# Where the side projection's matmul steps are dealt inside a DeltaNet head

## The chip, the cores and the metric

The kernel runs on one core of a Trainium2 chip. The metric is the device time of one execution in microseconds; the kernel before takes 2391.67 us, the median of three runs (2391.39 to 2391.86).

## The reference, cut to what matters

One layer of a hybrid trunk over 128 context tokens and 1024 latent tokens, D_MODEL = 1024, all in float32. One input projection feeds a pooling mixer, merge gates and a bidirectional chunked gated DeltaNet with 8 heads of width 128; an expert mixture with 16 experts follows. The change lies in the DeltaNet heads:

```python
decay = jnp.exp(jnp.where(incl, g[..., :, None] - g[..., None, :], -jnp.inf))
k_beta = k * beta[..., None]
lmat = jnp.where(strict, jnp.einsum('bhnck,bhnsk->bhncs', k_beta, k) * decay, 0.0)
a = lmat + jnp.eye(CHUNK, dtype=jnp.float32)
rhs = jnp.concatenate([v * beta[..., None], k_beta * jnp.exp(g)[..., None]], axis=-1)
sol = lax.linalg.triangular_solve(a, rhs, left_side=True, lower=True, unit_diagonal=True)
...
def step(S, inp):
    u_c, w_c, q_c, k_c, attn_c, d_c = inp
    v_new = u_c - jnp.einsum('bhck,bhkv->bhcv', w_c, S)
    o_c = (jnp.einsum('bhck,bhkv->bhcv', q_c, S) + jnp.einsum('bhcs,bhsv->bhcv', attn_c, v_new))
    S = S * d_c[..., None, None] + jnp.einsum('bhck,bhcv->bhkv', k_c, v_new)
    return S, o_c
```

The triangular solve is done in the kernel by inverting a unit triangular 128x128 matrix of each of 9 token tiles, in each direction, by block doubling.

## The kernel before, in words

The program is written by hand for each engine and synchronised by semaphores. After a prologue (adaLN, norms, the first head's projections) there are eight DeltaNet heads, seven in a hardware loop and a last one with its own table, then output projections, merge and the experts.

A head has two kinds of TensorE (PE) work. The first is its own chain: L2 norms and transposes of q, k, v, the products k k and k q (L1016), the inversion, its correction ("res" and "fix"), and a scan of nine token tiles (L1080 to L1105). The second is side work that nothing of this head waits for until late: the projections of the next head's q, k, v and this head's gate (pairs "qv" and "kg"), and two tiles of the merge and pooling columns (pair "AB"). `project` is a generator that yields after each matmul of it. Such a yield is a step; a step over 512 columns is L823 and shows in the trace as two matmul records, a step over 128 columns is L809. A pair is cut into jobs: two of 128 columns and eight steps each (c0, c1), and seven of 512 columns and four steps each, run in the order 1, 2, 6, 7, 5, 4, 3. Of these 1, 6, 7, 3 are copied out of PSUM by ScalarE (ACT, L863) and 2, 5, 4 are added by VectorE (DVE, L871), at the places where `evac` and `add` stand in those engines' programs. A job may begin only when the job before the last has left its bank.

`fill(place)` in `body_pe` runs as many steps as belong to a place. `FILL` gives each place a budget in units of 512 columns, and `steps_until` turns the running sum into step counts. The order of the places is the order of the program; the number of steps in all, 132 in a loop head and 156 in the last, is fixed, and what the budgets leave is run at the last place, "end2".

The inversion goes through six levels, b = 2, 4, 8, 16, 32, 64. The nine tiles stand in three groups g = 0, 1, 2, each with a PSUM bank of its own for either direction. On PE a level is, in float16:

- for each g a product Z (L1031, three matmuls) and, above the first level, a transpose X (L1023, three); then `fill("Z{b}_{g}")`;
- for each g a product P (L1031, three); then `fill("P{b}_{g}")`.

Z of group g waits for `low_changed` of the level below (L1043), X waits for `up_changed`, and P waits for ACT's copies of Z and X (L1209). DVE closes the level with nine operations in a fixed order: join 0 (L1402, reads P of group 0 from PSUM), to_low 0 (L1409), join 1, to_up 0 (L1414), to_low 1, join 2, to_up 1, to_low 2, to_up 2. Ahead of join 0 stands `add("Z{b}_2")`, which adds every sum job that is complete by that place. to_low g releases Z of the next level, to_up g releases X.

At a head's end the last scan tile is followed by `fill("end1")`, `fill("end2")`, and then nine transposes (L1124) of the normed output, which wait for DVE's L1497. The chain to it is: ACT drains the outputs, GpSimd (POOL) adds and squares them (L1598, L1600), DVE adds the jobs of "end1" and reduces (L1495), ACT takes a logarithm and an exponential, DVE multiplies (L1497). ACT then applies Silu to the gate (L1271) and copies job AB3. The first step of the next head waits until AB3 is copied (L787), and ACT goes on to the next head's Silu (L1145), from which the next head's chain runs through DVE's L1387 to the transposes L1023 that open the inversion ("Y2").

Of the kernel before, what the change touches and what calls it, by code (L numbers as in the profile page):

```python
# [19 lines left out]
P = 128  # L20
# [28 lines left out]
LEVELS = (2, 4, 8, 16, 32, 64)  # L49
# [29 lines left out]
def build(nc, a, out_p, out_s, out_sf, out_sb, dbg=None, stop=99):  # L79
    ctx = ExitStack()  # L80
    with ctx:
# [75 lines left out]
        qT, kT, vT, gateT = qkvg  # L157
# [516 lines left out]
            return [job_cols(job) for job in order for _ in range(job_steps(job))]  # L674

        UNIT = 512
        FILL = {"start": 4, "nk": 2.75, "qT": 4, "kk": 4, "Y20": 1, "Y21": 0.5, "Y22": 0.5, "X0": 1, "X1": 1, "X2": 1, "res": 2, "fix": 4, "end1": 5.5}
        FILL |= {f"{x}{b}_{g}": 0 if b in LEVELS[:3] and (x, g) == ("P", 2) else 1 for b in LEVELS for x in "ZP" for g in range(3)}
        FILL |= {f"scan{t}{x}": 1 for t in range(1, NT) for x in "abc"}
        FILL_LAST = FILL | {"start": 5, "Y20": 3, "Y21": 3, "Y22": 2, "fix": 4, "end1": 8}  # L680
        FILL_LAST |= {f"scan{t}{x}": 2 if x == "b" else 1 for t in range(1, NT) for x in "abc"}
# [3 lines left out]
        def steps_until(order):  # L685

            cols, budget, n, at = step_cols(order), 0.0, 0, {}
            for place in PLACES:
                budget += UNIT * (FILL if order is ORDER else FILL_LAST).get(place, 0)
                while n < len(cols) and sum(cols[:n + 1]) <= budget:  # L690
# [2190 lines left out]
```

## Time and profile before

| | |
|---|---|
| median of 3 runs | 2391.67 us (2391.39 to 2391.86) |
| the profiled execution | 2394.42 us, its span 2392.7 us |
| PE busy | 2302.0 us, 96% |
| DVE, ACT, POOL busy | 1101.9, 932.4, 380.4 us |
| a loop head (seven of them) | 132.7 us |
| the last head | 149.6 us |
| granted clock of PE, mean | 0.989 |

The profiled execution is 2.75 us above the median of the runs. A busy share of 96% for PE says little by itself: the ends of matmuls are modelled, so that a short wait between two groups may not show as idle time. The starts of the rows are the surer reading. All times below are from the start of the span.

### The profile page before, as it was taken

What the parts mean: (1) busy time and instruction counts of PE and PEld (TensorE: products, weight loads), DVE (VectorE), ACT (ScalarE), POOL (GpSimd) and SP (SyncE); (2) the same over time, 40 slices, a digit from 0 to 9 for tenths busy, and PEclk for the clock granted to TensorE, in tenths of its full rate; (3) what the DMA queues carried; (4) which work ended last, traced back from release to release, by engine and by line L of the source; (5) the groups of instructions that cost most, each with busy time, mean ns of one, the idle gap of its engine ahead of it and who ended that gap; (6) DMA issues with size and microseconds to landing.
All of it is one profiled execution on the core that took longest, in us unless ns stands there. A gap on an engine that the chain in (4) does not pass through costs nothing.

```text
span 2392.7 us, 39733 instructions
## 1 busy us (share of the span) xinstructions
PE 2302.0 (96%) x14208; PEld 1684.7 (70%) x14208; DVE 1101.9 (46%) x2161; ACT 932.4 (39%) x2437; POOL 380.4 (16%) x270
## 2 busy tenths in 40 slices
PE   6999999999999999999999999779999999999997
PEld 3456566665756666665644444569999999999997
DVE  3587776868686776866235316720010000100003
ACT  4173746555473747455311123213222232222323
POOL 1040413122230404132100000001001010010101
PEclk9999999999999999999999999979999999999999
DMA  9610212120201202121342422368877888778885
GB/s 346 253 47 22 68 38 69 35 72 18 86 21 42 61 24 69 29 70 40 143 161 99 159 79 106 121 219 294 295 250 261 281 293 296 250 260 282 293 291 213
DMA packets 198882, 362.31 MB, mean 151 GB/s; under 512 B 9082, under 2 KB 72519, under 8 KB 195723
## 3 DMA queue, kind: packets, MB, share of 16 engines
q1 hardware_dynamic: 191994, 341.73, 41.0%
q0 software_dynamic: 6528, 19.47, 3.1%
q8 instruction: 36, 0.59, 0.1%
q14 instruction: 51, 0.42, 0.1%
q10 hardware_dynamic: 273, 0.11, 0.0%
HBM read 320.63 MB, written 40.65 MB: 151 GB/s over the span
## 4 chain that ended last, share of the span: by engine, by line
PE 87%; DVE 5%; issue 3%; ACT 3%; DMA 1%; DVEq 0%; SPq 0%; ACTq 0%; POOLq 0%; POOL 0%
PE bank L823 22%; PE bank L2537 21%; PE bank L2551 11%; PE bank L2150 5%; PE bank L1887 5%; PE bank L1031 3%; PE bank L801 3%; PE bank L1905 2%; PE bank L1023 2%; PE bank L1089 2%; PE bank L809 1%; PE bank L1100 1%; PE bank L1105 1%; PE bank L1104 1%; PE bank L1080 1%
## 5 line engine op out<-in xcount | busy, mean ns | idle before, releaser
L823 PE MATMUL bank<-arena 128*128 128x512 f32 x1344 | 675.4, 606 | 0.0
L2537 PE MATMUL bank<-arena 128*128 128x144 f32 x4096 | 514.2, 286 | 3.1 <-ACT arena L2571 3.1
L2537 PEld LDWEIGHTS bank<-arena 128*128 128x128 f32 x4096 | 510.9, 190 | 3.2 <-ACT arena L2571 3.2
L2644 DVE TENSOR_TENSOR arena<-arena,bank 128x144 f32<-128x144 f32 x128 | 39.2, 306 | 698.9 <-ACT arena L2585 698.9
L823 PEld LDWEIGHTS bank<-arena 128*128 128x128 f32 x1344 | 217.0, 191 | 88.8 <-issue 87.5
L2551 PE MATMUL bank<-arena 128*128 128x144 f32 x2048 | 257.3, 286 | 0.7 <-DVE arena L2644 0.7
L2551 PEld LDWEIGHTS bank<-arena 128*128 128x128 f32 x2048 | 253.8, 189 | 1.9 <-DVE arena L2644 0.9
L2585 ACT ACTIVATE arena<-bank 128x144 f32<-128x144 f32 x128 | 37.5, 293 | 461.7 <-PE bank L2537 461.7
L1031 PEld LDWEIGHTS bank<-arena 128*128 128x128 f16 x1296 | 96.4, 98 | 156.4 <-issue 137.7
L1209 ACT ACTIVATE arena<-bank 128x384 f16<-128x384 f16 (+1 forms) x360 | 159.8, 491 | 90.0 <-PE bank L1031 67.9
L863 ACT ACTIVATE arena<-bank 128x128 f32<-128x128 f32 (+1 forms) x156 | 75.9, 491 | 169.5 <-PE bank L823 107.7
L1294 DVE SCALAR_TENSOR_TENSOR arena<-arena 128x1156 f32<-128x1156 f32 x96 | 136.1, 1417 | 1.3
L2150 PE MATMUL bank<-arena 128*128 128x512 f32 x288 | 128.7, 601 | 4.1 <-DVE arena L2044 2.1
L1303 POOL TENSOR_TENSOR arena<-arena 128x512 f32<-128x512 f32 x68 | 94.7, 1401 | 188.8 <-DVE arena L1512 60.4
L1031 PE MATMUL bank<-arena 128*128 128x128 f16 x1296 | 120.8, 219 | 1.9 <-DVE arena L1409 1.9
L1242 ACT ACTIVATE arena<-bank,arena 128x128 f32<-128x128 f32 x144 | 53.5, 371 | 151.4 <-PE bank L1089 151.4
L1887 PE MATMUL bank<-arena 128*128 128x512 f32 x256 | 110.6, 592 | 1.3 <-DVE arena L1510 1.3
L1402 DVE CAST_PREDICATED arena<-arena,bank 128x384 f16<-128x384 uint32 x144 | 79.7, 553 | 64.1 <-PE bank L1031 64.1
L2150 PEld LDWEIGHTS bank<-arena 128*128 128x128 f32 x288 | 53.8, 192 | 68.5 <-issue 66.4
L809 PEld LDWEIGHTS bank<-arena 128*128 128x128 f32 x768 | 92.4, 191 | 8.9 <-issue 6.2
L1409 DVE COPY_PREDICATED arena<-arena 128x384 f16<-128x384 uint32 x144 | 94.7, 657 | 6.9 <-DVE arena L1402 0.9
L809 PE MATMUL bank<-arena 128*128 128x128 f32 x768 | 97.7, 276 | 0.0
(327 smaller groups left out, 3038.3 us busy)
## 6 DMA issues: line engine op xcount, KB each, us to landing
arena<-in_exp_w_gate SPq DMA_DIRECT2D x32, 2048.0 KB, 10.6
arena<-in_exp_w_up SPq DMA_DIRECT2D x32, 2048.0 KB, 15.5
arena<-in_exp_w_down SPq DMA_DIRECT2D x32, 2048.0 KB, 10.8
arena<-in_w_in SPq DMA_DIRECT2D x52, 512.0 KB, 5.3
arena<-in_ada_w SPq DMA_DIRECT2D x24, 1024.0 KB, 8.1
side_dram<-arena SPq DMA_DIRECT2D x20, 576.0 KB, 4.2
arena<-g_dram SPq DMA_DIRECT2D x16, 576.0 KB, 4.2
arena<-in_x_sample SPq DMA_DIRECT2D x16, 512.0 KB, 6.0
```

The source lines that it names most:

```text
L809: ins = nc.tensor.matmul(bank[:, 0:CTX], weights_of(name)[:, k, :], hT3[:, k, 0:CTX], start=(k == 0), stop=(k == KD - 1))
L823: ins = nc.tensor.matmul(bank[:, 0:LH], w[:, k, :], x[:, k, :], start=(k == 0 and job[2] in "127"), stop=(k == KH - 1), skip_group_check=( ...
L1031: last = nc.tensor.matmul(TRI[d][g][:, i * P:(i + 1) * P], lhs[:, 3 * g + i, :], rhs[:, 3 * g + i, :], start=(n == 0), stop=(n == len(term ...
L1209: nc.scalar.activation(flat(dst, g), src[:, 0:384], ACT.Copy).then_inc(sem(f"drained{d}_act"), 1)
L1294: ins = nc.vector.scalar_tensor_tensor(conv_to[j][:, 0:CW], raw[j][:, tap:tap + CW], w, conv_to[j][:, 0:CW], ALU.mult, ALU.add)
L1303: unit.tensor_tensor(out, x, y, op).then_inc(sem("sums_ready"), 1)
L1402: nc.vector.copy_predicated(up[:, 3 * g:3 * g + 3, :], masks[:, 0, lv + 1, :].unsqueeze(1).to_broadcast([P, 3, P]), TRI[1][g][:, 0:384].re ...
L1409: nc.vector.copy_predicated(low[:, 3 * g:3 * g + 3, :], rows, up[:, 3 * g:3 * g + 3, :]).then_inc(sem("low_changed"), 1)
L1887: last = nc.tensor.matmul(banks[n % RING][:, 0:CH], w_dn[half][:, k, col:col + P], bT3[:, k, CTX + c * CH:CTX + (c + 1) * CH], start=(k == ...
L2150: last = nc.tensor.matmul(banks[2 * (i % 2) + half][:, 0:512], mixT3[:, k, t * P:(t + 1) * P], w_outs[:, k, half * 512:(half + 1) * 512], ...
L2537: last = nc.tensor.matmul(banks[3 + f % 2][:, m * CAP:(m + 1) * CAP], w_unit[2 * half + m][:, k, col:col + P], xsT[:, k, :], start=(k == 0 ...
L2551: last = nc.tensor.matmul(banks[5 + dt % 2][:, 0:CAP], w_unit[4 + half][:, k, col:col + P], hid[:, k, :], start=(k == 0), stop=(k == KD - 1))
```

## The change

Only the table `FILL` changes, and with it `FILL_LAST`, which is built from it. At the six levels the budgets per group go from 1, 1, 1 at Z to 0, 1, 2 (1, 0, 2 at b = 16), and at P from 1, 1, 1 (1, 1, 0 at b = 2, 4, 8) to 0, 2, 1 (0, 2, 0 at b = 8 and 0, 2, 2 at b = 64). "kk" goes from 4 to 5. A loop head then has run 86 steps instead of 82 when its scan begins, and "end2" holds 4 steps instead of 8; in the last head 5 instead of 9.

```diff
-        FILL = {"start": 4, "nk": 2.75, "qT": 4, "kk": 4, "Y20": 1, "Y21": 0.5, "Y22": 0.5, "X0": 1, "X1": 1, "X2": 1, "res": 2, "fix": 4, "end1": 5.5}
-        FILL |= {f"{x}{b}_{g}": 0 if b in LEVELS[:3] and (x, g) == ("P", 2) else 1 for b in LEVELS for x in "ZP" for g in range(3)}
+        FILL = {"start": 4, "nk": 2.75, "qT": 4, "kk": 5, "Y20": 1, "Y21": 0.5, "Y22": 0.5, "X0": 1, "X1": 1, "X2": 1, "res": 2, "fix": 4, "end1": 5.5}
+        FILL |= {f"Z{b}_{g}": n for b in LEVELS for g, n in enumerate((1, 0, 2) if b == 16 else (0, 1, 2))}
+        FILL |= {f"P{b}_{g}": n for b in LEVELS for g, n in enumerate((0, 2, 0) if b == 8 else (0, 2, 2) if b == 64 else (0, 2, 1))}
```

The new table is one line longer, so every line number behind it is higher by one in the changed kernel.

PE, loop head, from P of group 1 at b = 4 to X of group 1 at b = 8, in the kernel before (bank4 and bank5 hold P of groups 1 and 2, bank0 and bank1 hold Z, bank3 and bank4 hold X, bank7 the side steps):

```order
L1031 MATMUL bank4<-arena 128x128 x3
L823 MATMUL bank7<-arena 128x512
L1050 REGISTER_ALU
L631 REGISTER_ALU
L1031 MATMUL bank5<-arena 128x128 x3
L1043 ISA
L1031 MATMUL bank0<-arena 128x128 x3
L1023 MATMUL bank3<-arena 128x128 x3
L823 MATMUL bank7<-arena 128x512
L1043 REGISTER_ALU
L1031 MATMUL bank1<-arena 128x128 x3
L1023 MATMUL bank4<-arena 128x128 x3
```

The same stretch in the changed kernel:

```order
L1032 MATMUL bank4<-arena 128x128 x3
L824 MATMUL bank7<-arena 128x512 x2
L1051 REGISTER_ALU
L631 REGISTER_ALU
L1032 MATMUL bank5<-arena 128x128 x3
L750 REGISTER_ALU
L824 MATMUL bank6<-arena 128x512
L1044 ISA
L1032 MATMUL bank0<-arena 128x128 x3
L1024 MATMUL bank3<-arena 128x128 x3
L1044 REGISTER_ALU
L1032 MATMUL bank1<-arena 128x128 x3
```

Two steps now stand between P of groups 1 and 2 and one before Z of group 0, and none is left between X of group 0 and Z of group 1.

DVE, loop head, the end of level b = 4 and the begin of b = 8, before (L871 adds a sum job, here qv5, L1402 with bank3 is join 0 of b = 8):

```order
L1409 COPY_PREDICATED arena<-arena 128x384
L1414 COPY_PREDICATED arena<-arena 128x384
L868 REGISTER_ALU
L869 REGISTER_ALU
L871 TENSOR_TENSOR arena<-arena,bank7 128x512
L619 REGISTER_ALU
L1402 COPY_PREDICATED arena<-arena,bank3 128x384
```

and in the changed kernel:

```order
L1410 COPY_PREDICATED arena<-arena 128x384
L1415 COPY_PREDICATED arena<-arena 128x384
L869 REGISTER_ALU
L870 REGISTER_ALU
L872 TENSOR_TENSOR arena<-arena,bank7 128x512
L869 REGISTER_ALU
L870 REGISTER_ALU
L872 TENSOR_TENSOR arena<-arena,bank6 128x512
L1403 COPY_PREDICATED arena<-arena,bank3 128x384
```

Two sum jobs stand there now, qv5 (bank7) and qv4 (bank6); qv4 used to be added one level later. Its last step is now the last of `fill("Z8_2")`, the one directly ahead of P of group 0.

PE, end of a loop head, the changed kernel, from the last scan product to the transposes L1125:

```order
L1106 MATMUL bank5<-arena 128x128
L824 MATMUL bank7<-arena 128x512 x3
L750 REGISTER_ALU
L824 MATMUL bank6<-arena 128x512 x4
L822 REGISTER_ALU
L824 MATMUL bank7<-arena 128x512 x4
L1125 MATMUL bank0<-arena 128x128 x3
```

These are 11 steps (the ends of AB5, AB4 and AB3), where the kernel before has 15 at this place.

## Rows read from the trace of the kernel before

**Rows 1.** Page part 4 and stretches: us, then busy us (instructions) of each engine

```profile
PE 87%; DVE 5%; issue 3%; ACT 3%; DMA 1%; DVEq 0%; SPq 0%; ACTq 0%; POOLq 0%; POOL 0%
...
382.58:515.26 132.68, 130.81 (x759) 82.94 (x758) 98.93 (x180) 75.11 (x190) 34.64 (x22) 1.00 0.16 48
```

**Rows 2.** Stretches of that head, between starts of Y2, the levels' P, X, res

```profile
406.10:412.20 6.10, 6.07 (x37) 3.25 (x38) 5.03 (x9) 5.69 (x15) 4.11 (x4) 1.00 0.00 0
412.20:419.66 7.46, 6.61 (x38) 3.25 (x37) 5.45 (x9) 4.89 (x13) 2.33 (x4) 1.00 0.00 0
419.66:426.16 6.50, 6.44 (x38) 3.25 (x37) 5.18 (x10) 4.97 (x13) 1.05 (x1) 1.00 0.00 0
426.16:432.71 6.55, 6.47 (x38) 3.29 (x37) 5.08 (x10) 4.19 (x11) 2.27 (x2) 1.00 0.00 0
...
439.73:446.75 7.02, 7.02 (x40) 3.59 (x39) 6.23 (x11) 4.28 (x12) 2.91 (x2) 1.00 0.10 24
446.75:450.00 3.25, 3.25 (x16) 1.54 (x15) 2.81 (x5) 1.02 (x3) 2.09 (x1) 1.00 0.00 0
```

**Rows 3.** Timeline of PE: start us, us, engine, line, operation [idle before]

```profile
419.68 0.33 PE L1031 MATMUL bank<-arena 128*128 128x128 f16 x3
419.86 1.07 PE L823 MATMUL bank<-arena 128*128 128x512 f32 x2
420.77 0.33 PE L1031 MATMUL bank<-arena 128*128 128x128 f16 x3
...
423.82 0.34 PE L1023 MATMUL bank<-arena 128*128 128x128 f16 x3
...
456.03 1.94 PE L823 MATMUL bank<-arena 128*128 128x512 f32 x4
457.80 1.21 PE L1031 MATMUL bank<-arena 128*128 128x128 f16 x18
```

**Rows 4.** Timeline of DVE, levels 2 to 8 of that head

```profile
413.42 1.52 DVE L1409 COPY_PREDICATED arena<-arena 128x384 f16<-128x384 uint32 x1
...
420.17 0.56 DVE L1402 CAST_PREDICATED arena<-arena,bank 128x384 f16<-128x384 uint32 x1 [1.71 <-PE bank L1031]
...
421.81 0.56 DVE L1414 COPY_PREDICATED arena<-arena 128x384 f16<-128x384 uint32 x1
...
423.21 0.55 DVE L1414 COPY_PREDICATED arena<-arena 128x384 f16<-128x384 uint32 x1
...
424.38 0.56 DVE L1414 COPY_PREDICATED arena<-arena 128x384 f16<-128x384 uint32 x1
425.12 0.69 DVE L871 TENSOR_TENSOR arena<-arena,bank 128x512 f32<-128x512 f32 x1 [0.17 <-PE bank L823]
```

**Rows 5.** Timeline of POOL at the same place

```profile
413.26 1.27 POOL L1303 TENSOR_TENSOR arena<-arena 128x512 f32<-128x512 f32 x1
```

**Rows 6.** Timeline of PE, end of that head and begin of the next

```profile
502.19 13.05 PE L823 MATMUL bank<-arena 128*128 128x512 f32 x30
515.09 1.15 PE L1124 MATMUL bank<-arena 128*128 128x128 f32 x9
516.11 3.83 PE L809 MATMUL bank<-arena 128*128 128x128 f32 x32
...
538.80 0.51 PE L1023 MATMUL bank<-arena 128*128 128x128 f16 x6 [0.77 <-DVE arena L1387]
```

**Rows 7.** Timeline of DVE, the same

```profile
510.97 1.36 DVE L1497 TENSOR_TENSOR arena<-arena 128x1152 f32<-128x1152 f32 x1 [0.61 <-ACT arena L1264]
```

**Rows 8.** Timeline of ACT, the same

```profile
512.25 1.26 ACT L1271 ACTIVATE arena<-arena 128x128 f32<-128x128 f32 x2
515.29 0.60 ACT L863 ACTIVATE arena<-bank 128x512 f32<-128x512 f32 x1 [1.77 <-PE bank L823]
515.91 1.28 ACT L1145 ACT_TABLE_LOAD   x1
```

**Rows 9.** Waits of PE over six loop heads: us in all, times, longest

```profile
PE bank L1023 <- DVE arena L1387: 4.6, 6, 0.8
```

## The prediction

> **What bounds the kernel now.** I read the chain that ended last first: 87% of the span is PE [rows 1]. The number of matmuls doesn't change, so the time can only move through what lies between them. Then one loop head, cut into stretches: it lasts 132.68 us at a granted clock of 1.00 throughout [rows 1], and five of the six others last as long within 0.05 us; the first has the prologue ahead of it. Within it I cut at the start of each level's first P [rows 2]. A level with five steps takes 6.50 or 6.55 us, one with six takes 7.02 (two stretches alike, one shown), and the first boundary takes 7.46. Last I read PE and DVE row by row at those cuts, since the waits sit in the gaps between starts.
>
> **The units.** Fifteen steps in a row take 515.09 - 502.19 = 12.90 us, 0.86 each [rows 6]. A group of three float16 matmuls takes 419.86 - 419.68 = 0.18, and 0.17 where starts are compared over more groups; I use 0.17. A lone step between float16 groups takes 420.77 - 419.86 = 0.91, and two together 457.80 - 456.03 = 1.77 [rows 3]. So each interruption by steps costs about 0.05 us beside the steps, which is the one thing that dealing them in twos saves. A loop head's levels have 33 interruptions before and 23 after, a gain of 10 x 0.05 = 0.5 us, contained in the walks below.
>
> [...]
>
> **What the levels wait for.** DVE's nine operations start 0.49 us after P of group 0 starts (420.17 against 419.68) and run at a fixed pace. Counted from that start of P, to_up 0 ends at 421.81 + 0.56 - 419.68 = 2.69, to_up 1 at 4.08, to_up 2 at 5.26 [rows 3, 4]. X of group 1 starts at 423.82 - 419.68 = 4.14, 0.06 behind its release [rows 3]; by the same 0.06 X of group 0 can start at 2.75. Before, a five-step level already touches this chain, and a six-step level doesn't. X of group 2 can't start before 5.32.
>
> Now the walk of a changed level with six steps (0, 2, 1 at P and then 0, 1, 2 at Z). P0, P1, two steps, P2, one step, Z0, X0: X0 starts at 0.17 + 0.17 + 1.77 + 0.17 + 0.91 + 0.17 = 3.36, no wait. Z1 at 3.53, X1 would come at 3.70 and must wait until 4.14: 0.44 us, since the step that stood between X0 and Z1 is gone. Then 4.14 + 0.17 + 0.91 + 0.17 = 5.39 for X2, no wait, 5.56 its end, and two steps more before the next P0: 7.33 us. The two steps behind X2 are the point: P0 opens the next DVE chain, and they now stand in series with the old one.
>
> **Part by part, a loop head, net of steps at 0.86.** (A step run here isn't run at the end.)
> - Y2 to P of b = 2, five steps either way: walk 6.03 against 6.10, -0.07.
> - b = 2 to 4. POOL's L1303 stretches to_low 0 to 1.52 us, 0.96 more than its 0.56 [rows 4, 5]; both start as before, so X1 comes at 4.14 + 0.96 = 5.10. After: 5.10 + 0.17 + 0.91 + 0.34 + 1.77 = 8.29 with six steps, 3.13 net; before 7.46 - 4.30 = 3.16. -0.03.
> - b = 4 to 8: 7.33 - 5.16 = 2.17 against 6.50 - 4.30 = 2.20. -0.03.
> - b = 8 to 16, five steps. The add of qv4 now stands before join 0 and its last step ends only as P0 starts. An add starts about 0.20 behind its step (425.12, where the step behind X of 423.82 ends at 423.82 + 0.17 + 0.91 = 424.90) and DVE is free again some 0.60 later [rows 3, 4], so join 0 starts at 0.80 instead of 0.49 and X2 at 5.63. With 0, 2, 0 at P and 1, 0, 2 at Z, PE waits for DVE at X0, X1, Z2 and X2. 5.63 + 0.17 + 1.77 = 7.57, 3.27 net, against 6.55 - 4.30 = 2.25. +1.02. If the add hides wholly this is +0.7.
> - b = 16 to 32 and 32 to 64: 7.33 against 7.02, six steps both: +0.31 each.
> - P of 64 to X: three groups and four steps in two pairs, 4.05 - 3.44 = 0.61, against 3.25 - 2.58 = 0.67. -0.06.
>
> Sum +1.45 us a loop head, 10.2 for seven. Bounds: 0 each if every new wait is hidden (then -0.5 by the interruptions), 2.2 if each level still loses another 0.15. In the last head the walk is much the same, with more adds and longer POOL operations among the joins: 1.45, bounds -0.5 and +3.
>
> **The head's end.** L1497 ends at 510.97 + 1.36 = 512.33 [rows 7]; the steps end at 515.09, so the transposes wait for nothing [rows 6]. With 11 steps these end at 502.19 + 9.46 = 511.65. The add of AB4 joins that of AB5 before the reduction, but its last step is the seventh as AB5's was, so the reduction stays where it is. The transposes start at 512.38, a wait of 0.73, and end at 513.40. ACT's Silu of the gate ends at 513.51 [rows 8], the AB3 copy at about 514.05, and the next head's first step, which needs it, starts at 514.1 instead of 516.11: a second wait of 0.7. What is late next: ACT starts the next head at 514.07 instead of 515.91, 1.84 earlier, and before, the inversion opened on ACT's and DVE's chain with a 0.77 us wait [rows 6], six times 4.6 us together [rows 9]. So it opens at 538.80 - 1.84 = 536.96. PE, with one step more at "kk", gets there at 514.1 + (538.03 - 516.11) + 0.86 = 536.9: the old wait is used up. Net: 1.8 us earlier for three steps (2.58 us) fewer, +0.78, in six of the seven transitions. Into the last head, where PE had no such wait, the loss is whole: 3.44 saved at the end, 2.0 kept, +1.4. The first head loses a 0.28 wait: -0.3. At the last head's own end 14 steps stay before the transposes and cover the chain. Together 6 x 0.78 + 1.4 - 0.3 = +5.8 us. Bounds: -0.3 if the tail's chain moves forward with the steps, +9 if none of the old 0.77 is recovered.
>
> The scan keeps one budget unit per place; which places have the short steps moves by three, at equal columns. DVE's add of kg5 goes between "res" and "fix", where DVE idled 0.8 us; AB2's goes two tiles earlier, beside idle time. I cost both at nothing; uncovered, each is 0.6 us a head. Loads on SP's queue that follow a job are issued earlier or, at the end, up to 2 us earlier; nobody waits for them.
>
> **Sum.** 10.2 + 1.45 + 5.8 = +17.4 us on the profiled execution of 2394.42, 2411.8. The median is 2.75 below that execution, so 2409.1 for the median.
>
> **Rivals.**
> - *Only the levels.* The head's end is covered because the reduction moves forward. For it: POOL was done before the add. Against: the add waits for the same seventh step. 2391.7 + 11.4 = 2403.
> - *Only the head's end.* The levels' steps cover DVE wherever they stand, as the 7.02 us levels suggest with no wait at all. Against: X of group 1 starting 0.06 behind its release in level 4. 2391.7 + 5.8 - 8 x 0.5 = 2393.5, no change that can be measured.
> - *Faster.* Pairs run without gaps and DVE's chain isn't tied to P of group 0: with P0 and P1 back to back, join 0 and join 1 are ready together, and the chain is ahead by the time Z0 comes; all waits behind L1387, 4.6 us, go too. Place: the six levels; price: -0.5 a head and up to -1.0 of the gaps at the five-step levels; it decides if X of group 2 is released by 4.5 us instead of 5.26 after P0. 2391.7 - 8 x 0.5 - 4.6 = 2383. For it: X0 no longer waits at b = 4 and 8. Against: the nine operations already run without a gap once join 0 has started.
>
> **How the numbers follow.** Both parts as walked: 0.63, 2409, own range 2403 to 2415. Only the levels 0.12; only the end 0.08; faster 0.12; anything else 0.05. The range 2396 to 2415 holds the first two and part of the rest. A difference under 0.2%, 4.8 us, can't be told from none. Slower by more: 0.63 + 0.12 + some of the rest, 0.80; faster by more 0.13; within 0.07.
>
> **What would show it.** In the profile after: six-step levels of 7.33 us between starts of P0, with X of group 1 waiting 0.4 for L1415; 7.6 for b = 8 to 16, with an L872 between P0 and join 0; 0.7 us idle ahead of L1125 and again ahead of the next head's first step; no wait for L1388 ahead of the inversion; a loop head of about 134.9 us. Levels of 6.9 would refute the first part, a head's end with no idle PE the second.

## The result and the profile after

The changed kernel takes 2410.57 us (median of 4 runs, 2409.27 to 2412.11), the kernel before 2391.77 beside it (2391.39 to 2392.04). The ratio is 1.0078, interval 1.0064 to 1.0092: slower by 0.8%. The profiled execution of after is the run of 2409.27, its span 2407.5.

The chain of waits of this profile breaks off half way (PE has 50% of the span in it, against the 87% of [rows 1]), so I compare stretches. First the whole loop head and its levels, cut where [rows 1] and [rows 2] cut it: us, then busy us of PE, PEld, DVE, ACT and POOL (instructions), granted clock, DMA.

```profile
385.25:520.08 134.83, 130.86 (x758) 83.08 (x758) 100.49 (x180) 74.21 (x191) 33.53 (x22) 1.00 0.16 47
409.73:415.78 6.05, 6.05 (x38) 3.29 (x38) 5.04 (x9) 5.64 (x14) 4.06 (x4) 1.00 0.00 0
415.78:424.14 8.36, 7.43 (x40) 3.67 (x39) 5.50 (x9) 5.68 (x15) 2.37 (x4) 1.00 0.00 0
424.14:431.49 7.35, 7.09 (x40) 3.66 (x39) 5.08 (x10) 4.10 (x11) 1.90 (x1) 1.00 0.00 0
431.49:439.09 7.60, 6.67 (x38) 3.33 (x37) 5.09 (x10) 5.11 (x12) 2.15 (x2) 1.00 0.00 0
446.44:453.79 7.35, 7.08 (x40) 3.66 (x39) 6.54 (x11) 3.94 (x11) 2.73 (x2) 1.00 0.00 0
453.79:457.85 4.06, 4.06 (x18) 1.96 (x17) 3.93 (x6) 0.97 (x2) 0.66 (x1) 1.00 0.00 0
457.85:461.60 3.75, 3.75 (x25) 2.04 (x24) 3.60 (x6) 2.60 (x6) 0.00 (x0) 1.00 0.00 0
```

PE's busy time is the same as before (130.86 against 130.81), and 2.15 us were added to the head: all of it is waiting. A six-step level takes 7.35 where it took 7.02, and the one from b = 8 to 16 takes 7.60 with five steps where it took 6.55. The last row is X to "res": 3.75, where before it was 3.97 (450.00 to 453.97).

PE's timeline in levels 8 and 16, the rows that answer to [rows 3]; a wait stands in brackets:

```profile
428.31 0.34 PE L1024 MATMUL bank<-arena 128*128 128x128 f16 x3 [0.26 <-DVE arena L1415]
...
431.87 1.93 PE L824 MATMUL bank<-arena 128*128 128x512 f32 x4
433.64 0.51 PE L1032 MATMUL bank<-arena 128*128 128x128 f16 x6
434.59 0.34 PE L1024 MATMUL bank<-arena 128*128 128x128 f16 x3 [0.44 <-DVE arena L1415]
...
437.17 0.34 PE L1024 MATMUL bank<-arena 128*128 128x128 f16 x3 [0.36 <-DVE arena L1415]
```

The reader is to see that PE stands at X each time (L1024, released by to_up, L1415), that the wait printed at b = 8 comes right behind a Z with no step between, and that P of groups 0 and 1 is followed by two steps in one piece. The printed waits are short by the modelled ends: that Z started at 427.71, so X of group 1 stood for 428.31 - 427.71 - 0.17 = 0.43 us, the 0.44 of the walk. DVE at the same place ([rows 4] before; the first row is to_up 2, the end of the chain that began with P of b = 4 at 424.14):

```profile
428.87 0.56 DVE L1415 COPY_PREDICATED arena<-arena 128x384 f16<-128x384 uint32 x1
...
431.72 0.69 DVE L872 TENSOR_TENSOR arena<-arena,bank 128x512 f32<-128x512 f32 x1 [1.70 <-PE bank L824]
432.33 0.55 DVE L1403 CAST_PREDICATED arena<-arena,bank 128x384 f16<-128x384 uint32 x1
```

The add stands between P of group 0 (431.49) and join 0, which starts 0.84 behind P and not 0.49.

The head's end: PE, then DVE, then ACT ([rows 6 to 8] before).

```profile
520.08 1.20 PE L1125 MATMUL bank<-arena 128*128 128x128 f32 x9 [0.58 <-DVE arena L1498]
521.91 3.83 PE L810 MATMUL bank<-arena 128*128 128x128 f32 x32 [0.63 <-ACT arena L864]
...
544.60 0.51 PE L1024 MATMUL bank<-arena 128*128 128x128 f16 x6
```

```profile
518.66 1.36 DVE L1498 TENSOR_TENSOR arena<-arena 128x1152 f32<-128x1152 f32 x1 [0.61 <-ACT arena L1265]
```

```profile
519.94 1.26 ACT L1272 ACTIVATE arena<-arena 128x128 f32<-128x128 f32 x2
521.11 0.58 ACT L864 ACTIVATE arena<-bank 128x512 f32<-128x512 f32 x1
```

The transposes wait for DVE's multiply, the next head's first step waits for ACT's copy, and the inversion (544.60) opens without the wait that it had in [rows 6]. By starts the first of these waits is 0.74 us: the eleven steps start at 509.88 and need 9.46. PE's waits over six loop heads, in answer to [rows 9] (us in all, times, longest):

```profile
PE bank L1024 <- DVE arena L1415: 14.4, 42, 0.6
PE bank L1125 <- DVE arena L1498: 4.1, 7, 0.6
PE bank L810 <- ACT arena L864: 3.8, 6, 0.6
```

### The profile page after: what moved, and what is told of

Same layout as the page of the kernel before. It is cut to its first block, busy times and chain, and to the rows that moved or that the text cites. A ratio compares the mean times of both kernels' runs of the same rounds, so it can differ in the third digit from the quotient of the medians.

```text
span 2407.5 us, 39734 instructions
## 1 busy us (share of the span) xinstructions
PE 2300.5 (96%) x14208; PEld 1685.0 (70%) x14208; DVE 1113.8 (46%) x2161; ACT 925.8 (38%) x2437; POOL 373.4 (16%) x270
## 4 chain that ended last, share of the span: by engine, by line
PE 50%; DVE 1%; ACT 1%; issue 0%; DMA 0%; POOLq 0%; POOL 0%; DVEq 0%; ACTq 0%
PE bank L2538 21%; PE bank L2552 11%; PE bank L2151 5%; PE bank L1888 5%; PE bank L1906 2%; PE bank L824 2%; PE bank L2160 1%; PE bank L2508 1%; PE bank L2520 1%; DMA arena<-xn_dram,arena 0%; PE bank L1896 0%; PE bank L2178 0%; PE bank L2169 0%; DVE arena L2321 0%; PE bank L2512 0%
## 5 line engine op out<-in xcount | busy, mean ns | idle before, releaser
L824 PE MATMUL bank<-arena 128*128 128x512 f32 x1344 | 658.0, 602 | 0.0
L1032 PEld LDWEIGHTS bank<-arena 128*128 128x128 f16 x1296 | 91.0, 98 | 112.6 <-issue 95.2
L1295 DVE SCALAR_TENSOR_TENSOR arena<-arena 128x1156 f32<-128x1156 f32 x96 | 150.1, 1563 | 1.3
L2151 PE MATMUL bank<-arena 128*128 128x512 f32 x288 | 127.0, 595 | 4.1 <-DVE arena L2045 2.1
L1032 PE MATMUL bank<-arena 128*128 128x128 f16 x1296 | 113.5, 219 | 1.8
L1888 PE MATMUL bank<-arena 128*128 128x512 f32 x256 | 110.6, 592 | 1.3 <-DVE arena L1511 1.3
L1243 ACT ACTIVATE arena<-bank,arena 128x128 f32<-128x128 f32 x144 | 53.5, 371 | 128.7 <-PE bank L1090 128.7
L2151 PEld LDWEIGHTS bank<-arena 128*128 128x128 f32 x288 | 53.2, 189 | 67.5 <-issue 65.3
L2598 ACT ACTIVATE arena<-bank,arena 128x128 f32<-128x128 f32 x128 | 47.2, 369 | 128.5 <-PE bank L2552 128.5
```

Source lines behind the costliest of these rows:

```text
L824: ins = nc.tensor.matmul(bank[:, 0:LH], w[:, k, :], x[:, k, :], start=(k == 0 and job[2] in "127"), stop=(k == KH - 1), skip_group_check=( ...
L1032: last = nc.tensor.matmul(TRI[d][g][:, i * P:(i + 1) * P], lhs[:, 3 * g + i, :], rhs[:, 3 * g + i, :], start=(n == 0), stop=(n == len(term ...
L1295: ins = nc.vector.scalar_tensor_tensor(conv_to[j][:, 0:CW], raw[j][:, tap:tap + CW], w, conv_to[j][:, 0:CW], ALU.mult, ALU.add)
L1888: last = nc.tensor.matmul(banks[n % RING][:, 0:CH], w_dn[half][:, k, col:col + P], bT3[:, k, CTX + c * CH:CTX + (c + 1) * CH], start=(k == ...
L2151: last = nc.tensor.matmul(banks[2 * (i % 2) + half][:, 0:512], mixT3[:, k, t * P:(t + 1) * P], w_outs[:, k, half * 512:(half + 1) * 512], ...
```

## The experiments

Every kernel below differs from the kernel before by the lines shown, unless it says from the changed one. "A head" is the stretch between two starts of the transposes of the tail, the third and fourth heads' ends: 132.68 us before, 134.83 in the changed kernel.

**The deal alone.** The levels dealt in pairs, with the totals of before.

```diff
+        FILL |= {f"Z{b}_{g}": n for b in LEVELS for g, n in enumerate((0, 1, 2))}
+        FILL |= {f"P{b}_{g}": n for b in LEVELS for g, n in enumerate((0, 2, 0) if b <= 8 else (0, 2, 1))}
```

> Only the dealing is changed: Z 0, 1, 2 at every level, P 0, 2, 0 at b = 2, 4, 8 and 0, 2, 1 above, so every level has as many steps as before, and the head's end keeps its 8. Theory (P0 opens the next DVE chain, and the two steps behind X of group 2 stand in series with the old chain): the three five-step boundaries take as long as the six-step ones, about 7.3 us instead of 6.5 (b = 2 to 4: 8.3 instead of 7.5), +0.85 each, the two six-step ones 7.35 instead of 7.02, less about 0.1 elsewhere: +3.0 us a head, +24 for eight, about 2416. Rival (only the head's end costs): 2391.8 or, by the interruptions saved, 2388.

Measured: 2421.44 us, ratio 1.0126 (1.0110 to 1.0141). A head takes 135.59, 2.91 more, and the head's end is as before (its old 0.8 wait for L1388 is there six times). PE at b = 2 to 4 and on:

```profile
419.90 0.35 PE L1032 MATMUL bank<-arena 128*128 128x128 f16 x3 [0.37 <-DVE arena L1410]
420.83 0.34 PE L1024 MATMUL bank<-arena 128*128 128x128 f16 x3 [0.59 <-DVE arena L1415]
421.30 0.34 PE L1032 MATMUL bank<-arena 128*128 128x128 f16 x3
422.23 0.34 PE L1024 MATMUL bank<-arena 128*128 128x128 f16 x3 [0.59 <-DVE arena L1415]
```

So the deal by itself makes the levels slower, with no step added or taken. In three of the seven loop heads something came on top that the theory didn't have: another 1.65 us. PE's granted clock is the last figure but two of each row. The first row is from a head without the loss, the others from one with it:

```profile
419.41:422.41 3.00, 1.33 (x15) 0.70 (x13) 3.00 (x7) 1.69 (x4) 0.01 (x1) 1.00 0.00 0
...
555.00:558.00 3.00, 1.33 (x15) 0.70 (x13) 3.00 (x7) 1.70 (x4) 0.00 (x1) 1.00 0.00 0
...
560.00:561.00 1.00, 1.00 (x4) 0.48 (x3) 0.00 (x0) 1.00 (x3) 0.00 (x0) 0.50 0.00 0
...
562.00:565.00 3.00, 3.00 (x16) 1.38 (x16) 1.67 (x4) 0.60 (x1) 0.00 (x0) 1.00 0.00 0
```

PE was busy for 1.33 of 3.00 us while it waited for L1415, and then its clock was at 0.50 (the 1.2 GHz level) for some 3 us: two steps in a row took 2.88 us (559.98) against 1.94 at the full clock (563.04). Three times 1.65 us is about what this kernel is slower than the theory's figure. In the other four heads PE went through the same waits, to 0.01 us, and the clock stayed at 1.00 (the same two steps took 1.94 us at 423.67). So the waits alone don't decide it, and what does isn't shown.

**The totals alone.** One step per place throughout, 86 steps when the scan begins as in the changed kernel.

```diff
-        FILL |= {f"{x}{b}_{g}": 0 if b in LEVELS[:3] and (x, g) == ("P", 2) else 1 for b in LEVELS for x in "ZP" for g in range(3)}
+        FILL |= {f"{x}{b}_{g}": 1 for b in LEVELS for x in "ZP" for g in range(3)}
```

"kk" is 5 instead of 4 here too.

> The changed kernel's totals per head (36 steps in the levels, kk 5, four taken from the head's end), but dealt one at each of the 36 places. Theory: no level waits for DVE except the first (b = 2 to 4, stretched by POOL); boundaries of 7.0 us with six steps each, net of steps -1.5 us a head against before, -12 for eight, and the head's end +5.8 as in the changed kernel: about 2385.5, faster than before. Rival (the moved steps themselves cost, wherever they are dealt): like the changed kernel, 2410.

Measured: 2389.36 us, 0.9986 (0.9977 to 0.9995). A head takes 132.14: with the same 36 steps in the levels (one more between P of 8 and P of 16, one fewer behind P of 64), the even deal is 2.69 us a head and 21 us in all faster than the changed kernel. It missed its own figure by some 4 us. One cause is seen, and the rest stays open: POOL's attention multiply stretches to_low of group 0 at b = 64 to 1.61 us, where it took 1.31.

**The head's end alone.** Four steps from the end to "fix", the levels untouched.

```diff
-... "fix": 4, "end1": 5.5}
+... "fix": 8, "end1": 5.5}
```

> The levels as before; four steps of a loop head's end go to the place fix (4 to 8), kk stays 4. Theory of the head's end: the transposes wait about 0.6 and the next head's first step about 0.6, the next inversion opens 1.84 us earlier against 3.44 us of steps taken away, and nothing uses up the wait ahead of it: +1.6 us in six transitions and +1.4 into the last head, +11, 2403. Rival (the end is covered): 2391.8.

Measured: 2403.69 us, 1.0049 (1.0035 to 1.0062). A head takes 134.23, 1.55 more: 0.78 at the transposes, 0.78 at the next head's first step. The old wait at the inversion stays:

```profile
542.87 0.51 PE L1023 MATMUL bank<-arena 128*128 128x128 f16 x6 [0.76 <-DVE arena L1387]
```

**The same with one of the four at "kk".**

```diff
-"kk": 4, ... "fix": 4,
+"kk": 5, ... "fix": 7,
```

> As the run before, but one of the four steps goes to kk (5) and three to fix (7), as in the changed kernel. Theory: the step at kk uses the wait ahead of the inversion (0.77 us in six heads, 0.28 in the first): +0.78 x 6 + 1.4 - 0.3 = +5.8, 2397.6. Rival one: the end is covered, 2391.8. Rival two: the wait at the inversion isn't recovered, 2403 as the run before.

Measured: 2403.86 us, 1.0053 (1.0039 to 1.0067), a miss by 6 us, and the theory of the rival isn't right either. The wait at the inversion is gone as expected (24.51 us from the transposes to the inversion, 384.28 to 408.79, with a step more). The 0.8 us come back behind P of b = 64. The sum job kg2 is complete one place earlier, so DVE adds it at the end of b = 32, ahead of its convolution tap (L1294, a product and sum over 1156 columns for the next head's convolution). DVE and then POOL:

```profile
447.55 0.68 DVE L871 TENSOR_TENSOR arena<-arena,bank 128x512 f32<-128x512 f32 x1
448.14 3.42 DVE L1294 SCALAR_TENSOR_TENSOR arena<-arena 128x1156 f32<-128x1156 f32 x1
```

```profile
447.71 2.63 POOL L1581 TENSOR_TENSOR arena<-arena 128x1152 f32<-128x1152 f32 x1 [4.07 <-DVE arena L1414]
```

The tap starts 0.43 behind POOL's L1581, stands until about that one's end (450.34) and then takes its own 1.42 (the sum would be 3.62, 0.20 more than measured): join 0 of b = 64 is 1.6 late, 2.10 behind its P instead of 0.49. The next kernel tests this.

**Tap first.** The kernel just told, with DVE's two lines exchanged:

```diff
-                add(f"P{b}_2")
                 if lv >= 3:
                     tap()
+                add(f"P{b}_2")
```

> As the kernel with kk 5 and fix 7, but DVE does its convolution tap ahead of the add at the ends of levels 16, 32 and 64. There the add came first in level 32, the tap started 0.43 us behind POOL's L1581 and took 3.42 instead of 1.42 us. Theory (whoever of DVE and POOL starts first keeps the memory port, and the other stands still until it has finished): the tap starts 0.16 ahead of POOL and takes 1.42, join 0 of b = 64 is on time, 0.83 us a head come back in seven heads: 2403.9 - 5.5 = 2398.4. Rival: the 0.77 us at the inversion's start was never to be won, something else in the chain takes it: 2403.9.

Measured: 2398.06 us, 1.0025 (1.0016 to 1.0034). Forecast 2398.4. A head takes 133.38. The tap and POOL's L1581:

```profile
445.82 1.42 DVE L1294 SCALAR_TENSOR_TENSOR arena<-arena 128x1156 f32<-128x1156 f32 x1
```

```profile
445.99 3.74 POOL L1581 TENSOR_TENSOR arena<-arena 128x1152 f32<-128x1152 f32 x1 [4.05 <-DVE arena L1414]
```

Now DVE starts 0.17 ahead, and POOL is the one that is stretched, from 2.63 to 3.74. The order of two operations on one engine, 0.4 us apart, is worth 5.8 us. The Trainium skill ("SBUF — State Buffer", "🔬 SBUF: two separate sides") says that the pair of ports shared by DVE and GpSimd is an exclusive lock: a DVE operation with two SBUF inputs, as this tap is, and a GpSimd operation that reads SBUF exclude each other, whichever starts first has the pair for the whole instruction, and the other fully blocks. The rows of the two kernels agree, from both sides, within 0.2 us.

**Changed kernel, levels made even.** Same totals; P of 8 to 0, 2, 1, Z of 16 to 0, 1, 2, P of 64 to 0, 2, 1. From the changed kernel:

```diff
-enumerate((1, 0, 2) if b == 16 else (0, 1, 2))
+enumerate((0, 1, 2))
-enumerate((0, 2, 0) if b == 8 else (0, 2, 2) if b == 64 else (0, 2, 1))
+enumerate((0, 2, 1))
```

> The changed kernel with the same totals (41 steps in the levels), but P of b = 8 at 0, 2, 1, Z of b = 16 at 0, 1, 2 and P of b = 64 at 0, 2, 1: every level from b = 8 on has six steps in the same order. Theory (a level lasts as long as X of group 1 or 2 is held by DVE, plus what stands behind it): the b = 8 to 16 level loses its wait at X2 because a step now covers it, X of group 1 waits 0.7 instead; walked, 0.4 us a head less, 2407 in all. If it is only the count of steps that matters: 2410.6, unchanged. If the pairs themselves are the cost: 2410.6 or above, since there is one more pair followed by a lone step.

The levels hold 36 steps in both kernels; the 41 of the expectation count the five of "kk" with them. Measured: 2408.74 us, 1.0068 (1.0054 to 1.0082). A head takes 134.38, 0.45 less than in the changed kernel (forecast 0.4); over the whole kernel the difference, 1.8 us, is within the intervals of the two. In the 8 to 16 level PE has one printed wait:

```profile
435.03 0.34 PE L1024 MATMUL bank<-arena 128*128 128x128 f16 x3 [0.59 <-DVE arena L1415]
```

**Changed kernel, qv4's add behind the joins.**

```diff
-                add(f"Z{b}_2")
+                if last_h or b != 8:
+                    add(f"Z{b}_2")
                 join(0)
```

> The changed kernel, with the add of qv4 at b = 8 to 16 moved behind the joins of b = 16 (loop heads only). Theory: the add ahead of join 0 costs 0.31 us a head, so 2410.6 - 7 x 0.31 = 2408.4, and the idle time ahead of X in that level falls to the 0.44 of the other levels. Rival one: the add hides wholly in DVE's gaps, unchanged at 2410.6. Rival two: the bank that qv4 holds comes free some 5 us later and a side step waits for it, 2412 or more.

The expectation says "behind the joins of b = 16", but the edit is at b = 8: the add leaves its place between P of 8 and join 0 and comes behind the nine operations of the same level, at 436.41. Measured: 2406.91 us, 1.0061 (1.0047 to 1.0075). A head takes 134.55, and the 8 to 16 level 7.29 where it took 7.60: the 0.31 us of the walk. Over the whole kernel it is 3.7 us, forecast 2.2, and the intervals of the two kernels overlap. No side step waited for the bank.

```profile
431.22:438.51 7.29, 6.67 (x39) 3.33 (x37) 5.08 (x10) 5.06 (x12) 2.14 (x2) 1.00 0.00 0
```

**A better table, first attempt.** Six steps at b = 2 and 8 too, and the tap first as in "Tap first": 84 steps when the scan begins.

```diff
-"kk": 4, ... "fix": 4,
+"kk": 5, ... "fix": 3,
-0 if b in LEVELS[:3] and (x, g) == ("P", 2) else 1
+0 if b == 4 and (x, g) == ("P", 2) else 1
```

> The kernel before with kk 5 and fix 3, the missing step put in at P of group 2 of b = 2 and b = 8 (only b = 4 stays at five steps), one step per place everywhere else, and DVE's tap ahead of its add. 84 steps when the scan begins, 6 in end2. Theory: six-step levels with ones need 7.02 us and no wait, so the two filled levels win their waits, 1.17 us a head by the walk, and the step at kk wins the 0.77 at the inversion's start in six heads; 13 steps at the head's end still cover the chain there. 2392.2 - 8 x 1.17 - 6 x 0.77 = 2378, say 2375 to 2384. Rival one: the head's end has no room for two steps fewer, 0.8 a head are lost there, 2384 or more. Rival two: to_low of group 0 at b = 64 is stretched by POOL more than before (as with ones everywhere, 1.61 instead of 1.31 us), 0.25 a head lost, 2380.

Measured: 2391.22 us, 0.9996 (0.9987 to 1.0005), a miss by 13 us. PE's waits over six loop heads:

```profile
PE bank L823 <- DVE arena L871: 6.3, 6, 1.1
PE bank L1100 <- DVE arena L1455: 3.8, 6, 0.6
PE bank L1100 <- ACT arena L1243: 1.7, 6, 0.3
```

All waits at X and at the inversion are gone, as walked, and three new ones stand elsewhere, 2 us a head. A side step waits for kg2's bank, since the add now stands behind the tap; two adds stand between "fix" and the scan, ahead of L1455; and a place in the scan whose single step is a short one (0.22 us) doesn't cover ACT. None is a matter of how many steps a level has. All three come from which job ends at which place.

**Second attempt.** Six steps at b = 2 only, so 83 when the scan begins; otherwise as the first.

```diff
-"kk": 4, ... "fix": 4,
+"kk": 5, ... "fix": 3,
-0 if b in LEVELS[:3] and (x, g) == ("P", 2) else 1
+0 if b in LEVELS[1:3] and (x, g) == ("P", 2) else 1
```

> The kernel before with kk 5, fix 3, the missing step put in at P of group 2 of b = 2 alone, and DVE's tap ahead of its add: 83 steps when the scan begins, 7 in end2. In v1 (84 steps) two waits came in that the walk didn't have: a side step waited 1.05 us for the add of kg2 behind the tap, and the scan lost 0.9 us because two adds stand between fix and the remainder of tile 1 and a single short step stands ahead of L1100. With 83 steps kg4's add falls in the scan again, the short step stands elsewhere, and kg2's bank is wanted 1.25 us later. Theory: none of the three losses is there; per loop head 0.92 is won at b = 2 to 4 and 0.77 at the inversion's start, a loop head lasts 131.0 instead of 132.68; 2391.9 - 7 x 0.92 - 6 x 0.77 = 2380.8. Rival (such gains are always taken back by the next thing on the chain): 2388 or more.

Measured: 2382.24 us, 0.9957 (0.9943 to 0.9971): faster than both kernels, 9.7 us less than before and 28 less than the changed one. The profile lists no wait of PE over the six loop heads, and a head takes 131.11, forecast 131.0:

```profile
379.14:510.25 131.11, 130.86 (x758) 82.99 (x757) 99.17 (x180) 74.56 (x190) 34.64 (x22) 1.00 0.16 49
```

**Pairs at P, ones at Z.** As the second attempt, but P 0, 2, 1 (0, 2, 0 at b = 4 and 8).

```diff
+        FILL |= {f"Z{b}_{g}": 1 for b in LEVELS for g in range(3)}
+        FILL |= {f"P{b}_{g}": n for b in LEVELS for g, n in enumerate((0, 2, 0) if b in LEVELS[1:3] else (0, 2, 1))}
```

> As v2_step_at_2_kk5_fix3, but the two steps of P of groups 0 and 1 stand together behind group 1 (0, 2, 1 at P; 0, 2, 0 at b = 4 and 8) and Z keeps 1, 1, 1. Theory (what costs in the changed kernel is that two steps stand behind X of group 2 and none between X of 0 and X of 1, not that steps stand in pairs): no wait is added, and one interruption of 0.05 us a level is saved, 0.25 to 0.3 us a head, 2 us in all less than v2: 2379. Rival (the pairs at P delay or disturb DVE's chain as much as those at Z): the six-step levels of 7.3 us come back, 2385 or more.

Measured: 2381.42 us, 0.9960 (0.9947 to 0.9974), a head 131.07. Pairs at P cost nothing that can be measured. A six-step level takes 6.96 (429.06 to 436.02) where it takes 7.02 in the second attempt (430.53 to 437.55), which is the interruption saved; most of it is lost again at X, 0.16 at b = 4 and about 0.2 behind b = 64, and the whole is no measurable gain.

**Taps at b = 8, 16 and 64.** Against the last kernel two things differ: the levels that have a tap, and the order of tap and add, which is again that of the kernel before. The expectation speaks of the first alone.

```diff
-                if lv >= 3:
-                    tap()
                 add(f"P{b}_2")
+                if lv in (2, 3, 5):
+                    tap()
```

> As v4_pairs_at_P_ones_at_Z, but DVE's three taps within the levels stand at the ends of b = 8, 16 and 64 instead of 16, 32 and 64, so that POOL's L1581 meets no tap at b = 32 and is done before to_low of b = 64. Theory: L1581 takes 2.6 instead of 3.7 us, to_low of group 0 at b = 64 0.56 instead of up to 1.6, and the tap of 1.42 us at b = 16 starts just ahead of POOL's L1574 and holds it up without harm; what X waited for at b = 64 (0.2 to 0.6 us a head) is won, up to 3 us less than v4. Rival: at b = 16 POOL starts first and the tap takes 4 us, 2 us a head lost at b = 32.

Measured: 2389.54 us, 0.9990 (0.9981 to 0.9999): 8.1 us slower than the last, where up to 3 less were forecast. At the end of b = 8 POOL also has an attention multiply, L1582, which I had not looked at, and there the tap comes second, behind an add. POOL, then DVE:

```profile
430.24 2.63 POOL L1582 TENSOR_TENSOR arena<-arena 128x1152 f32<-128x1152 f32 x1 [4.28 <-DVE arena L1415]
```

```profile
429.99 0.68 DVE L872 TENSOR_TENSOR arena<-arena,bank 128x512 f32<-128x512 f32 x1
430.82 2.67 DVE L1293 TENSOR_SCALAR arena<-arena 128x1156 f32<-128x1156 f32 x1
```

The first tap, 0.82 us elsewhere, takes 2.67, and X of the next level waits 0.69. It is the third case of a DVE operation held by one of POOL, on another pair of operations. With the tap ahead of the add it could have started at 429.99, 0.25 us ahead of POOL. That kernel was not run, so this result doesn't show that the end of b = 8 is a bad place for a tap; it shows the order of tap and add once more. At b = 16, where no add stood there, the tap was first (438.18 against 438.35) and took 1.42. The hoped-for part came: to_low of group 0 at b = 64 took 0.72 us (448.02) where it took 1.37 in the last kernel (444.16).

## Why the prediction was right

The forecast was 2409 with 2396 to 2415, the measured median 2410.57. It was right by its steps: both mechanisms came as walked, and all terms but one within 0.07 us. Terms of a loop head, net of steps at 0.86 us, in the order of the prediction:

| term | walked | measured |
|---|---|---|
| Y2 to P of 2 | -0.07 | 6.05 - 6.10 = -0.05 |
| 2 to 4 | -0.03 | (8.36 - 5.16) - (7.46 - 4.30) = +0.04 |
| 4 to 8 | -0.03 | 2.19 - 2.20 = -0.01 |
| 8 to 16 | +1.02 | 3.30 - 2.25 = +1.05 |
| 16 to 32, 32 to 64 | +0.31 each | 7.35 - 7.02 = +0.33 each |
| P of 64 to X | -0.06 | 0.62 - 0.67 = -0.05 |
| X to "res" | none | 3.75 - 3.97 = -0.22 |
| levels in all | +1.45 | +1.42 |
| end, per transition | +0.78 | 0.79 - 0.05 = +0.74 |

The end: the scan's stretch to the transposes has 4 steps fewer and 0.79 us lost, and from there to the inversion 24.52 us instead of 23.71, with one step (0.86) more.

The seven loop heads and the last head together are 17.2 us longer (the last transposes start at 1209.7 instead of 1193.1, and the first side step of the heads at 113.97 instead of 114.51), where 17.4 were forecast. This sum is closer than its parts. The first head got 1.21 us longer where its terms give 1.9, the stretch from the seventh head's transposes to the last head's got 2.95 longer (150.28 against 147.33) where they give 2.1, and these two misses cancel by luck; the six between got 13.0, forecast 13.4. Most of the first head's miss is that POOL held to_low of b = 2 for less time there, 1.11 us (147.80) against 1.57 in a later head (417.00): X of group 1 came 4.69 us behind P (151.30 against 146.61) and not 5.15. The profiled execution as a whole is 14.9 longer; the medians are 18.8 apart. The rest of the program, which the change doesn't touch, differs by up to 2 us between executions.

**The levels.** That two steps behind X of group 2 stand in series with the next chain is shown by three kernels. The deal alone costs 2.91 us a head at equal totals, the even deal with the new totals is 2.69 faster than the changed one, and pairs at P alone cost nothing that can be measured. So the deal at Z does it (two steps behind X of group 2 and none behind X of group 0, which are the same step moved), and the rival "only the head's end" falls. In the changed kernel part of what the deal costs is paid for by steps: three of its places have one more step than before.

**8 to 16.** The share of qv4's add, 0.31 us, was measured by moving it (7.60 to 7.29), and the pair in series by making the level even.

**The head's end.** The experiment with four steps at "fix" shows both waits without any change in the levels, 1.55 us a head; the changed kernel pays half, since its step at "kk" uses up the old wait at the inversion. "Only the levels" falls.

**Faster** falls in each part: X of group 2 was released 5.29 us behind P of group 0 (428.87 + 0.56 - 424.14), not by the 4.5 that this rival needed, and the even deal beats the changed one, so the pairs had no gap to save but the 0.05 us of each interruption. That price holds (6.96 against 7.02).

**What the prediction lacked.** Three things, none large here.
- X to "res" got 0.22 shorter, which nearly makes up for what the other level terms were short. The cause is read from the rows and was not tested. Before, L1581 stretched to_low of group 0 at b = 64 to 1.31 us; in the changed kernel POOL starts first, the tap is stretched to 3.42 us instead (452.25), and the two pairs of steps behind P hide that. I saw POOL's hold on DVE at b = 2 and didn't follow it to b = 64.
- In the last head the walk's 1.45 was 2.3 (67.5 us from inversion to scan with three steps more, instead of 62.7).
- The place of DVE's adds was costed at nothing, or 0.6 us a head uncovered. In the changed kernel that held. In two of the experiments the same sort of shift cost 0.85 and 1.7 us a head (the latter without the 0.3 that ACT's part took): an add that moves by one place moves what stands behind it past the start of a POOL operation, or keeps a bank.

Open is why the clock fell in three of seven heads that had the same waits. That the scan's loss in the first attempt comes from the two causes named rests on its profile alone.

## What to carry to other kernels

Filler work belongs inside a chain that another engine runs, between what starts it and what ends it. A step behind the last release stands in series with the next chain; the same count of steps was worth 21 us of 2390 by its place alone. After every shift of a schedule, read what ends where on the other engines: here a job that completed one place earlier moved DVE's tap behind a POOL operation and took back the whole gain. Where an operation of one engine holds up one of another, put first the one on which the chain hangs (here DVE's tap, which is also the shorter), and look at every place where the other runs, not only at the one that was in the way.

## Behaviour of the hardware not expected

- A DVE operation that starts just behind a POOL one is held for all of it: 3.42 us for a tap of 1.42 (POOL's L1581, 2.63), 2.67 for one of 0.82. With DVE 0.17 us ahead POOL takes 3.74 instead. DVE's joins and adds, which read a bank of PSUM, ran beside POOL at their usual 0.56 and 0.68 us (in the kernel before an add at 446.26 and a join at 447.25, beside POOL's L1581 of 445.10 to 448.84), where to_low, which reads none, was held to 1.31 (447.94).
- Waits can cost more than their length, and not each time. In the kernel with the deal alone PE was busy 1.32 or 1.33 of 3.00 us in all seven loop heads, and behind that its granted clock was 0.50 for some 3 us in three of them and 1.00 in four. In the changed kernel, where PE was busy 7.43 of the 8.36 us of that level, the clock stayed at 1.00 in every stretch shown. In the first head, behind a wait of 2.59 us that both kernels have, the clock was 1.00 in the profile of before and 0.50 in that of the changed kernel (the two rows, before and changed). The matmuls behind it took 3.66 us instead of 2.02 (starts 120.30 to 123.96 against 120.84 to 122.86), and two waits that stood behind them before, 1.31 and 0.28 us, were gone:

```profile
122.00:124.00 2.00, 2.00 (x14) 1.52 (x13) 1.16 (x3) 1.98 (x4) 1.41 (x2) 1.00 1.21 290
```

```profile
122.00:124.00 2.00, 2.00 (x4) 0.72 (x3) 1.51 (x3) 1.98 (x2) 1.77 (x2) 0.50 1.21 290
```

- A group of float16 matmuls that float32 steps interrupt costs 0.05 to 0.06 us each time (levels of 7.02 and 6.96 with the same work).
